# Last four output tiles finished one after another, and the sparse-attention loop re-sequenced on four engines

## The reference

```python
def dsa_attention(aq, ak, av, iq, ik, iw):          # 4 query heads, one key/value head
    ...
        _, idx = lax.top_k(score, k_top)             # k_top = 128 of 512 keys
        ...
        logits = jnp.einsum("bqhd,bqkd->bhqk", qb, kg).astype(jnp.float32) * scale
        logits = jnp.where(valid[:, None], logits, -jnp.inf)
        p = jax.nn.softmax(logits, axis=-1).astype(vg.dtype)
        return jnp.einsum("bhqk,bqkd->bqhd", p, vg)
...
        hm = head_rms_norm(hm, g_mlstm_head[l]).reshape(B, S, M_WIDTH)
        hm = (jax.nn.sigmoid(mo.astype(jnp.float32)) * hm).astype(x.dtype)
        y = jnp.concatenate([hm, ha], axis=-1) @ w_out[l]
        x = x + gt1 * rms_norm(y, g_mix_post[l])
        h2 = rms_norm(x, g_ffn_pre[l]) * (1.0 + sc2) + sh2
        y2 = moe_ffn(h2, ...)                        # 64 experts, top 8, and one shared
        x = x + gt2 * rms_norm(y2, g_ffn_post[l])
```

## Time and profile before

| | us |
|---|---|
| median of 3 runs | 1054.93 (1053.38 to 1056.37) |
| profiled execution | 1055.45 |
| its span, first to last instruction | 1053.6 |
| PE busy | 988.6 (94%) |
| DVE busy | 912.1 (87%) |
| ACT busy | 684.6 (65%) |
| mean granted TensorE clock | 0.985 of full speed |

### The profile page before, as it was taken

One profiled execution on the slowest core, in us unless ns is written; L12 is line 12 of the kernel. 1 busy time (PEld: TensorE's weight loads), 2 busy tenths in 40 slices (PEclk: granted clock), 3 DMA queues, 4 the chain that ended last, 5 costly groups with the idle time before them and its releaser, 6 DMA issues.

```text
span 1053.6 us, 15339 instructions
## 1 busy us (share of the span) xinstructions
PE 988.6 (94%) x5065; PEld 780.7 (74%) x5066; DVE 912.1 (87%) x1266; ACT 684.6 (65%) x742; POOL 202.9 (19%) x144
## 2 busy tenths in 40 slices
PE   0899999978999999999999999999999999999986
PEld 0898889756546547888888888878878878878874
DVE  3888899878576747999999999999999999999984
ACT  2524365465222137888888888888888888888862
POOL 0000000100000031222322322322334233333310
PEclk9899999998999999999999999999999999999998
DMA  9776210330594539999999999999999999999932
GB/s 353 284 256 227 83 42 1 118 143 1 197 376 154 205 111 373 349 374 378 380 374 385 367 374 366 374 366 381 366 371 360 380 367 382 377 378 379 315 85 96
DMA packets 89333, 296.25 MB, mean 281 GB/s; under 512 B 17185, under 2 KB 29645, under 8 KB 79821
## 3 DMA queue, kind: packets, MB, share of 16 engines
q1 hardware_dynamic: 69476, 259.18, 63.6%
q0 software_dynamic: 18304, 33.60, 13.0%
q10 hardware_dynamic: 1514, 2.97, 0.8%
HBM read 289.39 MB, written 39.32 MB: 312 GB/s over the span
## 4 chain that ended last, share of the span: by engine, by line
PE 40%; DVE 12%; issue 10%; ACT 2%; DVEq 0%
PE ps L2099 23%; PE ps L2157 9%; PE ps L2089 4%; DVE w_down_lo L1968 3%; DVE xT_lo L1950 2%; DVE w_gate_up_lo L1946 2%; ACT w_gate_up_hi L1816 2%; PE ps L2117 2%; DVE pick L1928 1%; PE ps L2107 1%; DVE uT_lo L1959 1%; DVE u L1955 1%; PE ps L2175 0%; DVE pad L1602 0%; DVE xt L2073 0%
## 5 line engine op out<-in xcount | busy, mean ns | idle before, releaser
L1946 DVE TENSOR_TENSOR w_gate_up_lo<-side,w_gate_up_hi 128x2048 fp32r<-128x2048 f32 x64 | 146.3, 2286 | 11.7 <-ACT w_gate_up_hi L1816 9.3
L1613 POOL DMA_INDIRECT y_rows<-yb,row_numbers x62 | 120.9, 1950 | 184.3 <-DMA y_rows<-yb,row_numbers 124.3
L1946 DVE TENSOR_TENSOR w_gate_up_lo<-main,w_gate_up_hi 128x2048 fp32r<-128x2048 f32 x64 | 146.4, 2288 | 5.4 <-ACT w_gate_up_hi L1816 3.4
L2099 PE MATMUL ps<-w_gate_up_hi,xT_hi 128*128 128x512 f32 x512 | 144.4, 404 | 6.1 <-DVE xT_lo L1950 5.2
L2099 PE MATMUL ps<-w_gate_up_hi,xT_lo 128*128 128x512 f32 x512 | 137.5, 390 | 0.0
L2099 PE MATMUL ps<-w_gate_up_lo,xT_hi 128*128 128x512 f32 x512 | 137.0, 389 | 0.0
L1816 ACT ACTIVATE w_gate_up_hi<-side 128x2048 fp32r<-128x2048 f32 x64 | 122.3, 1912 | 5.7 <-PE ps L2099 3.7
L1816 ACT ACTIVATE w_gate_up_hi<-main 128x2048 fp32r<-128x2048 f32 x64 | 122.5, 1914 | 2.6 <-PE ps L2099 2.3
L2099 PEld LDWEIGHTS ps<-w_gate_up_hi,xT_hi 128*128 128x128 f32 x512 | 91.2, 188 | 29.0 <-issue 12.5
L2099 PEld LDWEIGHTS ps<-w_gate_up_hi,xT_lo 128*128 128x128 f32 x512 | 96.1, 188 | 21.0
L2099 PEld LDWEIGHTS ps<-w_gate_up_lo,xT_hi 128*128 128x128 f32 x512 | 96.1, 188 | 20.4
(11 more groups left out here) (319 smaller groups left out, 1808.9 us busy)
## 6 DMA issues: line engine op xcount, KB each, us to landing
side<-in_w_exp_gate SPq DMA_DIRECT2D x60, 512.0 KB
side<-in_w_exp_up SPq DMA_DIRECT2D x60, 512.0 KB
main<-in_w_exp_gate SPq DMA_DIRECT2D x60, 512.0 KB
main<-in_w_exp_up SPq DMA_DIRECT2D x60, 512.0 KB
side<-in_w_ada SPq DMA_DIRECT2D x20, 1024.0 KB, 7.7
main<-in_w_exp_down SPq DMA_DIRECT2D x16, 1024.0 KB
maskb<-in_w_exp_down SPq DMA_DIRECT2D x16, 1024.0 KB
side<-in_w_exp_down SPq DMA_DIRECT2D x16, 1024.0 KB
```

Source lines behind the costliest of these rows:

```text
L1613: return pool.indirect_dma_start(out=G.y_sums, out_offset=bass.IndirectOffsetOnAxis(ap=sidx[:, n:n + 1], axis=0), in_=yb[:, slot, :], in_o ...
L1946: nc.vector.tensor_tensor(wlo[:, half], src, whi[:, half].bitcast(F32), ALU.subtract).then_inc(s_wlo, 1)
L2099: ins = nc.tensor.matmul(ps[0:CAP, 2 + slot, :], xp[:, HALF * half + c, :], wp[:, half, c].rearrange("p m f -> p (m f)"), start=half == 0 ...
```

## The change

In the attention stage: ACT does the squares of head 2 only, then a one-element Exp; the squares of head 3 move behind `copy_pT(0)` and the Sqrt into round 5 (`ROOT_AT`). `choose_last` moves to rounds 1 to 4, its close to round 5. The norm, turn and copy of the recurrent heads move from rounds 1 to 4 to rounds 9 to 12 (`HEADS_AT`), and use bank 2. Logits use two banks, 0 and 1. PE's list per round becomes `turn(u)`, `logits(u+2)`, `attend(u-1)`. `copy_out` moves from DVE to ACT.

In the experts' stage: the last expert's down product goes to banks 6 and 7 and no longer waits for `s_yl`; tiles 1 and 3 swap bank pairs; and PE finishes tile 0 (both experts and the sums), then 1, 2 and 3, where it had done the first expert's part of tiles 0 to 2, then the second's.

```diff
--- before.py
+++ after.py
@@ -770,7 +770,7 @@
         var = sb("var", [P, HEADS, NT])
         rstd = sb("rstd", [P, HEADS, NT])
         mx = sb("mx", [P, 2])
-        rsum = sb("rsum", [P, 2])
+        rsum = sb("rsum", [P, 3])
         rinv = sb("rinv", [P, 2])
         dinv = sb("rinv_diagonal", [P, 2, P])
         sqb = sb("sqb", [P, NT, DH])
@@ -805,7 +805,9 @@
         s_o = sem("attended")
         s_od = sem("attended_copied")
         UNITS = [(h, i) for i in range(NT) for h in range(HEADS)]
-        LAST_ROUNDS = (5, 6, 7, 8)
+        LAST_ROUNDS = (1, 2, 3, 4)
+        HEADS_AT = 8
+        ROOT_AT = 5
         SCALE = DH ** -0.5
         ROW_BANK = [6, 7, 6, 7]
         s_clear = sem("row_cleared")
@@ -859,10 +861,8 @@
                 if h >= 2:
                     head_squares(h - 2)
             nc.scalar.activation(nat[:, :, O0:O0 + 512], nat[:, :, O0:O0 + 512], ACT.Sigmoid).then_inc(s_sig, 1)
-            for h in range(2, HEADS):
-                head_squares(h)
-            act.wait_ge(s_hsq, 1)
-            nc.scalar.activation(rstd[:, :, :], var[:, :, :], ACT.Sqrt).then_inc(s_hrt, 1)
+            head_squares(2)
+            nc.scalar.activation(rsum[:, 2:3], k[:, K_ONES:K_ONES + 1], ACT.Exp)
             act.wait_ge(s_num, HEADS)
 
             def exp_unit(u):
@@ -882,18 +882,31 @@
                     act.wait_ge(s_o, u - 1)
                 nc.scalar.activation(prT[:, u % 2, 0:w], ps[:, 3 + u % 3, 0:w], ACT.Copy).then_inc(s_pTd, 1)
 
+            def copy_out(i):
+                act.wait_ge(s_o, HEADS * (i + 1))
+                nc.scalar.activation(catT[:, HEADS:2 * HEADS, i * P:(i + 1) * P],
+                                     ps[:, 6 + i % 2, :].rearrange("p (h t) -> p h t", h=HEADS), ACT.Copy).then_inc(s_od, 1)
+
             def copy_head(h):
 
                 act.wait_ge(s_hT, h + 1)
-                nc.scalar.activation(catT[:, h, :], ps[:, 7, :], ACT.Copy, scale=cols[:, 40 + h:41 + h]).then_inc(s_hTd, 1)
+                nc.scalar.activation(catT[:, h, :], ps[:, 2, :], ACT.Copy, scale=cols[:, 40 + h:41 + h]).then_inc(s_hTd, 1)
 
             for u in range(len(UNITS)):
                 exp_unit(u)
                 if u:
                     copy_pT(u - 1)
-                if 2 <= u < HEADS + 2:
-                    copy_head(u - 2)
+                if u == 1:
+                    head_squares(3)
+                if u == ROOT_AT:
+                    act.wait_ge(s_hsq, 1)
+                    nc.scalar.activation(rstd[:, :, :], var[:, :, :], ACT.Sqrt).then_inc(s_hrt, 1)
+                if 2 <= u - HEADS_AT < HEADS + 2:
+                    copy_head(u - HEADS_AT - 2)
+                if u >= HEADS + 2 and (u - 2) % HEADS == 0:
+                    copy_out((u - 2) // HEADS - 1)
             copy_pT(len(UNITS) - 1)
+            copy_out(NT - 1)
 
         @block.vector
         def _(dve):
@@ -962,8 +975,6 @@
                 if h:
                     read_head(h - 1)
             read_head(HEADS - 1)
-            dve.wait_ge(s_vsq, HEADS)
-            nc.vector.tensor_scalar(var[:, :, :], var[:, :, :], 1.0 / DH, EPS, ALU.mult, ALU.add).then_inc(s_hsq, 1)
 
             def norm_head(h):
 
@@ -984,7 +995,7 @@
                 dve.wait_ge(s_lg, u + 1)
                 if u >= 2:
                     dve.wait_ge(s_ex, u - 1)
-                nc.vector.tensor_tensor_reduce(out=lg[:, u % 2, 0:w], in0=ps[:, u % 3, 0:w], in1=maskb[:, i, 0:w], scale=-SCALE,
+                nc.vector.tensor_tensor_reduce(out=lg[:, u % 2, 0:w], in0=ps[:, u % 2, 0:w], in1=maskb[:, i, 0:w], scale=-SCALE,
                                                scalar=-FMIN, op0=ALU.add, op1=ALU.min,
                                                accum_out=mx[:, u % 2:u % 2 + 1]).then_inc(s_lgd, 1)
 
@@ -997,15 +1008,13 @@
                 dve.wait_ge(s_ri, u + 1)
                 nc.vector.tensor_scalar(dinv[:, u % 2, :], ident, rinv[:, u % 2:u % 2 + 1], None, ALU.mult).then_inc(s_pn, 1)
 
-            def copy_out(i):
-                dve.wait_ge(s_o, HEADS * (i + 1))
-                nc.vector.tensor_copy(catT[:, HEADS:2 * HEADS, i * P:(i + 1) * P],
-                                      ps[:, 6 + i % 2, :].rearrange("p (h t) -> p h t", h=HEADS)).then_inc(s_od, 1)
-
             for u in range(len(UNITS)):
                 mask_unit(u)
-                if 1 <= u <= HEADS:
-                    norm_head(u - 1)
+                if u == 3:
+                    dve.wait_ge(s_vsq, HEADS)
+                    nc.vector.tensor_scalar(var[:, :, :], var[:, :, :], 1.0 / DH, EPS, ALU.mult, ALU.add).then_inc(s_hsq, 1)
+                if 1 <= u - HEADS_AT <= HEADS:
+                    norm_head(u - HEADS_AT - 1)
                 if u:
                     invert(u - 1)
                 if u in LAST_ROUNDS:
@@ -1013,10 +1022,7 @@
                 if u == LAST_ROUNDS[-1] + 1:
                     step(nc.vector.tensor_tensor(G.last_left, G.last_left, maskb[:, NT - 1, :], ALU.is_equal))
                     step(nc.vector.tensor_scalar(maskb[:, NT - 1, :], G.last_left, NEG, None, ALU.mult))
-                if u >= HEADS + 2 and (u - 2) % HEADS == 0:
-                    copy_out((u - 2) // HEADS - 1)
             invert(len(UNITS) - 1)
-            copy_out(NT - 1)
 
         @block.tensor
         def _(pe):
@@ -1075,14 +1081,14 @@
                 if h:
                     pe.wait_ge(s_hTd, h)
                 for i in range(NT):
-                    ins = nc.tensor.transpose(ps[:, 7, i * P:(i + 1) * P], hall[:, i, h * DH:(h + 1) * DH], ident)
+                    ins = nc.tensor.transpose(ps[:, 2, i * P:(i + 1) * P], hall[:, i, h * DH:(h + 1) * DH], ident)
                 ins.then_inc(s_hT, 1)
 
             def logits(u):
                 h, i = UNITS[u]
-                if u >= 3:
-                    pe.wait_ge(s_lgd, u - 2)
-                nc.tensor.matmul(ps[:, u % 3, 0:P * (i + 1)].rearrange("p (j t) -> p j t", t=P), nat[:, i, AQ0 + h * DH:AQ0 + (h + 1) * DH],
+                if u >= 2:
+                    pe.wait_ge(s_lgd, u - 1)
+                nc.tensor.matmul(ps[:, u % 2, 0:P * (i + 1)].rearrange("p (j t) -> p j t", t=P), nat[:, i, AQ0 + h * DH:AQ0 + (h + 1) * DH],
                                  nat[:, 0:i + 1, AK0:AK0 + DH], start=True, stop=True).then_inc(s_lg, 1)
 
             def turn(u):
@@ -1098,8 +1104,6 @@
             def attend(u):
                 h, i = UNITS[u]
                 pe.wait_ge(s_pTd, u + 1)
-                if i == 1 and h == 0:
-                    pe.wait_ge(s_hTd, HEADS)
                 if i >= 2 and h == 0:
                     pe.wait_ge(s_od, i - 1)
                 for j in range(i + 1):
@@ -1111,13 +1115,13 @@
             logits(1)
             pe.wait_ge(s_numd, HEADS)
             for u in range(len(UNITS)):
+                turn(u)
                 if u + 2 < len(UNITS):
                     logits(u + 2)
-                turn(u)
                 if u:
                     attend(u - 1)
-                if 1 <= u <= HEADS:
-                    turn_head(u - 1)
+                if 1 <= u - HEADS_AT <= HEADS:
+                    turn_head(u - HEADS_AT - 1)
             attend(len(UNITS) - 1)
 
 
@@ -1664,7 +1668,7 @@
             s_sdc = isem("shared_copied")
             s_yw = isem("shared_stored")
             TURNS = E_N // UNROLL
-            LAST_BANK = [0, 6, 2, 4]
+            LAST_BANK = [0, 4, 2, 6]
             place = wdh[:, 0, :].rearrange("p (n t) -> p n t", n=2)
             ylast = [wdl[1], wdl[2]]
             xxT = G.main[:, 0:KC * P].rearrange("p (c t) -> p c t", c=KC)
@@ -1881,12 +1885,13 @@
                     if ahead(1) and not ahead(2):
                         uT_high(e + 1, (n + 1) % 2)
                     act.wait_ge(s_dn, e + 1)
+                    b = 4 if ahead(1) else 6
                     if ahead(2):
                         act.wait_ge(s_sc, 16 * e + (SC0 - 16))
                         rows_to = yb[:, n % 2, :].rearrange("p (a b) -> p a b", a=2)
                     else:
                         rows_to = ylast[n % 2][:, 0, :].rearrange("p (a b) -> p a b", a=2)
-                    nc.scalar.activation(rows_to, ps[0:CAP, 4:6, :], ACT.Copy, scale=found[:, n, 1:2]).then_inc(s_ya, 1)
+                    nc.scalar.activation(rows_to, ps[0:CAP, b:b + 2, :], ACT.Copy, scale=found[:, n, 1:2]).then_inc(s_ya, 1)
                     if ahead(1):
                         if ahead(2):
                             uT_high(e + 1, (n + 1) % 2)
@@ -2018,7 +2023,8 @@
                 def low_last(n):
                     e = E_N - UNROLL + n
                     dve.wait_ge(s_ya, e + 2)
-                    nc.vector.scalar_tensor_tensor(ylast[n % 2][:, 1, :], ps[0:CAP, 4:6, :].rearrange("p a b -> p (a b)"), found[:, n, 1:2],
+                    b = 4 if e < E_N - 1 else 6
+                    nc.vector.scalar_tensor_tensor(ylast[n % 2][:, 1, :], ps[0:CAP, b:b + 2, :].rearrange("p a b -> p (a b)"), found[:, n, 1:2],
```

(17 more changed lines are left out.)

## The result

| | before | after |
|---|---|---|
| median, us | 1055.41 (7 runs) | 1060.13 (7 runs) |
| ratio of after to before | | 1.0046 (1.0031 to 1.0061) |
| again, in the experiments' series | 1055.59 | 1060.39, ratio 1.0044 (1.0027 to 1.0061) |

The change makes the kernel about 4.8 us slower. The rows of after are from the second profiled execution of the changed kernel (1058.6 us of span), because the first one was disturbed in the experts' stage, as were the profiled ones of `tail_only`, `invert_first` and `lf_root_ahead`; of these only the attention loop and the tail are read, and all ratios go by undisturbed executions alone.

What follows compares the result with a forecast made beforehand. PE was taken to bound the old loop late, at about 2.4 us per width-512 unit, and waits the tail. Attention +6.1 (+5.1 plus 1 for clock) and tail -5.7 gave +0.4: 1055.4 us against the median, range 1051.5 to 1060.0.

Steps and rivals of the forecast that it cites:

- The case given 0.61: Whole kernel: attention's loss and the tail's gain, 5 to 6 us each, cancel to within about 0.3% (3.2 us).
- rival 1: Attention rounds 1 to 10: PE stays at 1.2 GHz, costing 2.5 to 3.6 us; time 1058 to 1061, chance 0.27.
- The tail: End of experts' stage: earlier down product at full clock, tiles every 3.58 us; gain 5.7 us, bounds 3.9 and 5.9.
- The loop's start: Start of attention loop: first Exp at 233.2 and first turn at 234.3, a gain of 3.65 us.
- Rounds 0 to 12: Attention loop, turn 0 to turn 12: 33.6 us against 26.5, so +7.1 us at full clock.
- the circle through mask and invert: Attention rounds: turn, logits, mask, invert, next turn run in line, 3.1 us per round at width 512.
- Rounds 12 to 16: Late attention loop: two circles of 3.1 us and one of 1.7, 7.9 against 6.0, so +1.9 us.
- The end: Attention, from turn 15 to the copied tile: 3.4 against 3.6 us with copy_out on ACT, so -0.2 us.
- The clock in the loop: Attention loop: PE's clock may fall in thinner rounds; 1 us allowed, between bounds of 0 and 3.6.
- the upper bound of 3.6 us: Attention loop: cost of PE's clock at 1.2 GHz in all of rounds 1 to 10.
- The forecast's own sign for the loop: End of attention: the last copy near 279 to 280 would show the forecast right.
- The table loads: ACT, round 5: root and two 1.28 us loads without the skill's drain, whose figure would add 2.8 us.

Runs made afterwards that it cites:

- tail_only: The kernel before with only the experts' stage (tail) edits; 1050.04 us, ratio 0.9955 to the kernel before.
- invert_first: The changed kernel, PE's order kept, with DVE's invert(u-1) put ahead of mask(u); 1048.63 us, ratio 0.9917 to the kernel before.
- lf_root_ahead: The changed kernel with logits(u+2) again before turn(u), and head 3's squares, root and Exp load back ahead of the loop; ratio 0.9948 to the kernel before.

## Why the prediction was wrong

1055.4 us was forecast, in a range of 1051.5 to 1060.0; 1060.13 was measured. The case given 0.61, that gain and loss cancel within 0.3%, did not come; rival 1, a low clock through much of the loop, with 0.27 and 1058 to 1061, did. Of the 4.7 us between forecast and measurement 2.9 are the clock's, and the rest is in the sizes of the other terms, most of them a little short.

- **The tail**: -5.7 forecast, -5.35 in the trace, -4.8 (0.9955) in the run of its own. Right, and by its steps: no wait for DVE, full clock, 3.6 us per tile. Two small sizes were off: 3.00 for 2.79 us of down product, and 0.16 us of wait before tile 0's second part (2.02 for 1.86 us).
- **The loop's start**: -3.65 forecast, 234.38 - 237.93 = -3.55 measured. Right.
- **Rounds 0 to 12**: +7.1 at full clock. Measured 38.31 - 26.51 = +11.8; with the clock held up by the fillers, 34.45 - 26.51 = +7.9. The mechanism, the circle through mask and invert, was right and is shown by three runs: undone on PE, undone on DVE, and done alone.
- **Rounds 12 to 16**: +1.9 forecast, 281.00 - 272.69 - 6.00 = +2.3. A turn that starts from a wait takes 1.00 to the next product, not 0.90, so a circle is 3.21 and not 3.1 us. This is also part of the 0.8 above.
- **The end**: -0.2 forecast, 3.54 against 3.63 us, -0.1.
- **The clock in the loop** is the step that failed: "I take 1, from the early rounds, where DVE hides most of PE's slowness". It cost 3.9 us. I kept DVE's hiding from the old rounds, but in a closed circle PE's turn and logits aren't beside DVE's work; they are in line with it, so a slower PE shows. Up to turn 2 the search on DVE still hid it (4.23 us from turn 0 with and without fillers); from turn 2 to 5 it cost 1.8 us and from turn 8 to 10 2.0. The run with the fillers in the open loop shows the other side: there a low clock of 10 us costs 0.5 us. And the mean of 0.74 in the old loop, with its 7 us at the lower level, was a warning that it might last longer in thinner rounds: it was about 20 us. Even the upper bound of 3.6 us, for which the forecast gives no working, was short of the 3.9, and the sum took 1. The forecast's own sign for the loop, a last copy near 279 to 280, came at 284.54.
- **The table loads.** The gaps behind the loads are 0.01 to 0.02 us, in the loop too, as the row had it. The forecast went by them and held: the 2.66 us per switch of the Trainium skill (ScalarE: Activation LUTs, "What ACT_TABLE_LOAD costs") are not seen here: root and two loads take 2.82 us together. With the root ahead of all of the loop's Exps, as that page advises ("Table sets: the hidden batching unit": all Exps together), the loop ended 1.3 us later (`lf_root_ahead`), since the Exp table's load ahead of the loop (231.84 to 233.12 in the changed kernel) lies nearly all in a wait for the last head and the first mask, which is ready at 232.88.

The sum with the measured sizes: -3.55 + 11.8 + 2.3 - 0.1 = +10.45 in attention, -5.35 in the tail, +5.1; measured +4.8.

## What to carry to other kernels

When two engines each hold a list of software-pipelined steps, walk the circle through both lists before moving one step in one of them: here a turn moved ahead of a product two units younger tied that product, the mask and the diagonal into one line, and PE and DVE waited for each other, ACT for both, with none of them full. In a closed circle nothing hides PE's work, at a low TensorE clock either (3.9 us for about 20 at the lower level here, 0.5 for 10 in the open loop), so a clock allowance must be made from whether PE's work is in line or beside other work. And a change with two halves behind barriers is to be measured by halves: the tail's half was a gain of 0.45%, and with the order on PE undone the whole change is one of 0.7%.

## What the runs showed that was not expected

Eleven products of 512 columns into an unused bank, read by nobody, made the loop 3.9 us shorter (ratio 1.0006, 0.9981 to 1.003, for 1.0044, 1.0027 to 1.0061), by holding the clock at 2.4 GHz through 50 us in which PE was busy 41.77 us, fillers included. Without them PE was busy 39.43 of 52.6 us, but at half speed in 20 of these, and so looked almost as busy. In the tail, 1.57 us of idle PE before the last down product did not bring the clock down in any of the nine profiles with the new tail (2.99 to 3.01 us for its 12 products); the 2.89 us before it in the three with the old tail did each time (4.49, 4.58 and 5.46 us). What brings it down exactly was not tried.
